# Second layer of the second block: part of the gated half's value projection moved from the input projection into the retention half, with the gate scratch moved

## Chip, cores and metric

One core of one Trainium2 chip. The metric is the device time of one execution in microseconds (us), median of the runs. The kernel computes two stacked transformer-like blocks on 256 latent tokens and 256 context tokens of width 1024; the change touches only the last layer of the second block, some 200 us before the end.

## The reference, cut to what matters

For each of its two layers the second block projects the normed tokens once (`h @ w_in`) and splits the result. Four parts feed the retention half (q, k, v and a gate branch), four the gated half (GLA: q, k, v, and a gate branch), two are low-rank gate inputs. The second layer needs no output for the context: its rows are wanted only where they feed the states.

```python
RET_W, GLA_K, GLA_V = 512, 256, 512
IN_SPLITS = (RET_W, RET_W, RET_W, RET_W, GLA_K, GLA_K, GLA_V, GLA_V, 16, 16)

def hybrid_mixer(h, hc, w_in, ...):
    lat = project_in(h, w_in)          # 256 latents
    cx = project_in(hc, w_in)          # 256 context rows
    ...
    def gla_inputs(parts):
        q = to_heads(parts[4], 4) * (64 ** -0.5)
        k = to_heads(parts[5], 4)
        v = to_heads(parts[6], 4)      # the value projection of the gated half
        a_f = to_heads(gla_log_gate(parts[8], gate_up[0], gate_b[0]), 4)
        a_b = to_heads(gla_log_gate(parts[9], gate_up[1], gate_b[1]), 4)
        return q, k, v, a_f, a_b

    r_lat, r_ctx = bidirectional_scan(retention_inputs(lat, True), retention_inputs(cx, False))
    g_lat, g_ctx = bidirectional_scan(gla_inputs(lat), gla_inputs(cx))
    return merge(r_lat, g_lat, lat), ...
```

## The kernel before

**Engines and order.** Each engine runs a program written out by hand, with semaphores between them. In layer `l` of the second block (`l` is 0 or 1, the second layer is `l == 1`) there are four phases: `l1_in` (input projection), `l1_att` (retention, then gated half), `l1_out`, `l1_mlp`. `phase_end` is a barrier of all five engines' programs except where it is told not to wait.

**Input projection.** `w_in` comes in chunks of 512 columns: chunk 0 is q, 1 is k, 2 is v, 3 the gate branch of retention, 4 q and k of the gated half, 5 its v, 6 its gate branch, and 7 the 32 low-rank columns. Products are made to nearly full precision from three matmuls of rounded operands (`mm3`: high times high, high times low, low times high). Latents and context stand side by side: `Hh` (high) and `Hl` (low, same memory as `H`) are 8 blocks of 128 features by 512 tokens, columns 0 to 255 the latents, 256 to 511 the context. Chunks 2 and 5 are made token-major: for each of four token blocks `tb` (0 and 1 are latents, 2 and 3 context) 8 x 3 matmuls of 512 columns go into one bank, and ScalarE (`take`) copies it to `RV` or `GV`. The other chunks are made feature-major, four tiles of 24 matmuls, 256 columns wide for the second layer, 512 where the context is wanted too.

**The ring.** Weights go through four slots of 2 MB. A chunk takes two: it lands in slot `n`, VectorE (`split_chunk`) casts it to the high part in slot `n+1` and writes the low part back into slot `n`, and TensorE then waits for the pair (`chunk_in`). When TensorE has used the pair, it adds 2 to the semaphore `used`; that count rides on the first matmul of the next chunk (`pend`). `load` on SyncE waits for `used` to reach `n - RING + 1`. So the load of a chunk is issued only once TensorE has begun the chunk before it, and lands and is split while that one is computed.

**Retention half.** Per head `h` (0 to 3): GpSimd makes decay arguments (`head_args`), ScalarE their exponentials (`head_exps`), VectorE scales (`head_prep`), TensorE makes the context state, scores of the next head, the intra product, the state's product and turns the next keys; ScalarE squares the head, TensorE sums it (`variance`), ScalarE and VectorE normalise. Between these stand the gate's soft-plus (`gate_soft`), its running sums (`gate_sums`, a scan), `end_exp` and `gate_exps`. TensorE runs its list in order, as all engines do. The buffers of the decay tables lie over `Hh`.

**Gated half.** `g_keys(0)` turns keys into banks 6 and 7, then scores, updates, masks, states and outputs of both directions. It reads `GV`.

Of the kernel before, what the change touches and what calls it, by code (L numbers as in the profile page):

```python
# [23 lines left out]
ALU = mybir.AluOpType  # L24
ACT = mybir.ActivationFunctionType
AX = mybir.AxisListType

P = 128
# [123 lines left out]
def build(nc, T, out):  # L152
    ctx = ExitStack()
    with ctx:
# [67 lines left out]
        END = MLP1 + 16  # L222
        WIN_ORDER = [1, 0, 3, 2, 4, 5, 6, 7, 8, 9, 10, 11]
# [70 lines left out]
        def _(sp):  # L294
# [199 lines left out]
        GT1 = [H[:, 2 * d:2 * d + 2, :] for d in range(2)]  # L494
        GLg = [H[:, 4 + 2 * d:6 + 2 * d, :] for d in range(2)]
        GQM, GQD = GT1, GLg
# [54 lines left out]
        def _(pe):  # L551
# [491 lines left out]
            for l, first, mlp in ((0, L0, MLP0), (1, L1, MLP1)):  # L1043
                W = 2 * L if l == 0 else L
                for j in range(7):
                    n = first + 2 * j
                    chunk_in(n + 1)
                    wh, wl = as_cols(n + 1, slot=low), as_cols(n, slot=low)
                    if l and j < 2:
                        wh = NextHigh(j)  # L1050
                    if j == 0:
                        o = [tile_bank() for nt in range(4)]
                        for k in range(KT):
                            if l:
                                pe.wait_ge(S("normed"), 56 + 2 * (k + 1))
                            else:
                                pe.wait_ge(S("h_split"), 8 + k + 1)
                            for nt in range(4):
                                for w in (wh, wl):
                                    mm(o[nt][:, 0:W], w[:, k, nt * P:(nt + 1) * P], Hh[:, k, 0:W], k == 0 and w is wh, False)  # L1060
                            if l:
                                pe.wait_ge(S("h_split"), 8 + 16 + k + 1)
                            for nt in range(4):
                                mm(o[nt][:, 0:W], wh[:, k, nt * P:(nt + 1) * P], Hl[:, k, 0:W], False, k == KT - 1,
                                   "tile_done" if k == KT - 1 else None)
                    elif j in (2, 5):
                        for tb in range(4):
                            o = tile_bank()
                            c = slice(tb * P, (tb + 1) * P)
                            for k in range(KT):  # L1070
                                mm3(o, (Hh[:, k, c], Hl[:, k, c]), (wh[:, k, :], wl[:, k, :]), k == 0, k == KT - 1,
                                    "tile_done" if k == KT - 1 else None)
                    else:
                        for nt in range(4):
                            wide = 2 * L if j == 1 or (j == 4 and nt >= 2) else W
# [16 lines left out]
                n = first + 14  # L1092
                chunk_in(n + 1)
                wh, wl = as_cols(n + 1, 32, slot=low), as_cols(n, 32, slot=low)
                o = tile_bank()
                for k in range(KT):
                    mm3(o[0:32, :], (wh[:, k, :], wl[:, k, :]), (Hh[:, k, :], Hl[:, k, :]), k == 0, k == KT - 1,
                        "tile_done" if k == KT - 1 else None)
                chunk_used(2)
# [19 lines left out]

                keys_turned(0)  # L1120
# [5 lines left out]
                for h in range(RT_H):  # L1126
# [42 lines left out]
                def g_scores(d, part):  # L1169
# [4 lines left out]
                    for ch in half_of(part):  # L1174
                        for h in range(4):
# [3 lines left out]
                               GQM[d][r, h // 2, ch * P:(ch + 1) * P], inc="g_scores" if h == 3 else None)  # L1179
# [15 lines left out]
                def g_inter(d):  # L1195
                    for n, ch in enumerate(order[d]):
# [3 lines left out]
                        for h in range(4):  # L1200
                            r = slice(64 * (h % 2), 64 * (h % 2) + 64)
                            mm(ps[h][:, ch * P:(ch + 1) * P], GST[d][r, n - 1, h // 2, :], GQD[d][r, h // 2, ch * P:(ch + 1) * P], False, (d, n) == (1, 3),
                               "g_out" if (d, n) == (1, 3) else None)

                g_keys(0)
# [142 lines left out]
        def _(act):  # L1348
# [281 lines left out]
            for l in range(LAYERS):  # L1630
# [13 lines left out]
                for j in range(8):  # L1644
                    for nt in range(1 if j == 7 else 4):
# [43 lines left out]
                def gate_out(d):  # L1689
                    for t in range(2):  # L1690
                        act.wait_ge(S("gate_mm"), 4 * l + 2 * d + t + 1)
                        A_(GT1[d][:, t, :], ps[(5, 1, 2, 3)[2 * d + t]][:, :], ACT.Identity, bias=vec("gate_b", l * 4 + d * 2 + t))\
# [12 lines left out]
                def gate_exps(d):  # L1705
                    link(A_(GKM[d], GT1[d], ACT.Exp, scale=-1.0 / 16))
                    A_(GQM[d], GT1[d], ACT.Exp, scale=1.0 / 16).then_inc(S("g_exp"), 1)
                    end = P - 1 if d == 0 else 0
                    link(A_(GEND[d], GLg[d].rearrange("p t (c k) -> p (t c) k", k=P)[:, :, end], ACT.Exp, scale=1.0 / 16))
                    A_(GQD[d], GLg[d], ACT.Exp, scale=1.0 / 16).then_inc(S("g_exp"), 1)  # L1710
# [20 lines left out]
                head_square(1)  # L1731
                head_exps(3)
# [6 lines left out]
                gate_exps(0)  # L1739
                head_inverse(2, 5)  # L1740
# [202 lines left out]
        def _(dve):  # L1943
# [448 lines left out]
            for l in range(LAYERS):  # L2392
# [68 lines left out]
                by_chunk = lambda a: a.rearrange("p t (c k) -> p (t c) k", k=P)  # L2461
# [11 lines left out]
                def gate_args(d):  # L2473
                    v = by_chunk(GLg[d])
                    mid, end = (63, 127) if d == 0 else (64, 0)
                    V.tensor_tensor(by_chunk(GT1[d]), v, bc(v[:, :, mid:mid + 1], [P, 8, P]), ALU.subtract)
                    V.tensor_tensor(by_chunk(GKE[d]), bc(v[:, :, end:end + 1], [P, 8, P]), v, ALU.subtract).then_inc(S("g_arg"), 1)
# [5 lines left out]
                def gate_products(d):  # L2483
# [3 lines left out]
                    V.tensor_tensor(GQM[d][:, :, 0:W], GQM[d][:, :, 0:W], GQ[:, :, 0:W], ALU.mult).then_inc(S("gq_ready"), 1)  # L2487

                def gate_queries(d):
                    dve.wait_ge(S("g_exp"), 3 * (2 * l + d) + 3)  # L2490
                    V.tensor_tensor(GQD[d][:, :, 0:W], GQD[d][:, :, 0:W], GQ[:, :, 0:W], ALU.mult).then_inc(S("gq_ready"), 1)
# [212 lines left out]
```

## Time and profile before

| | us |
|---|---|
| median of 3 runs | 1970.4 (1968.82 to 1971.67) |
| profiled execution, its own time | 1971.46 |
| its span in the trace | 1969.6 |
| TensorE busy | 1868.5 (95%) |
| VectorE / ScalarE / GpSimd busy | 818.2 / 586.1 / 387.5 |
| input projection of the second layer, TensorE's matmuls | 1553.1 to 1687.5 |
| retention half, first matmul to last variance but one | 1688.4 to 1717.2 |
| gated half, to the last output copied | 1717.2 to 1741 |

Times below are us from the span's start. The busy share of TensorE is an average over the whole program; in the retention and gated halves it is lower.

### The profile page before, as it was taken

What the parts mean: (1) busy time and instruction counts of PE and PEld (TensorE: products, weight loads), DVE (VectorE), ACT (ScalarE), POOL (GpSimd) and SP (SyncE); (2) the same over time, 40 slices, a digit from 0 to 9 for tenths busy, and PEclk for the clock granted to TensorE, in tenths of its full rate; (3) what the DMA queues carried; (4) which work ended last, traced back from release to release, by engine and by line L of the source; (5) the groups of instructions that cost most, each with busy time, mean ns of one, the idle gap of its engine ahead of it and who ended that gap; (6) DMA issues with size and microseconds to landing.
All of it is one profiled execution on the core that took longest, in us unless ns stands there. A gap on an engine that the chain in (4) does not pass through costs nothing.

```text
span 1969.6 us, 26164 instructions
## 1 busy us (share of the span) xinstructions
PE 1868.5 (95%) x11248; PEld 1366.6 (69%) x11248; DVE 818.2 (42%) x1342; ACT 586.1 (30%) x892; POOL 387.5 (20%) x205
## 2 busy tenths in 40 slices
PE   5999999999999999999999899999999899889998
PEld 2777796964444343447887657888888688679998
DVE  1615255731111111116343744566655625574333
ACT  2513103331111111113113535223333411544554
POOL 2000000120000000004003132333443210425665
PEclk8999999989999999999999899999999899999999
DMA  9479917669999999992224004454445222414451
GB/s 357 153 256 344 341 44 278 215 270 429 426 427 428 427 427 427 427 394 82 86 86 161 3 33 171 150 181 162 149 150 182 92 91 89 171 47 168 174 196 38
DMA packets 111425, 429.84 MB, mean 218 GB/s; under 512 B 5706, under 2 KB 8821, under 8 KB 98512
## 3 DMA queue, kind: packets, MB, share of 16 engines
q1 hardware_dynamic: 109056, 416.56, 54.5%
q0 software_dynamic: 2256, 11.62, 1.6%
q8 instruction: 90, 1.47, 0.3%
q14 instruction: 23, 0.19, 0.0%
HBM read 427.11 MB, written 1.05 MB: 217 GB/s over the span
## 4 chain that ended last, share of the span: by engine, by line
PE 65%; DMA 17%; DVE 5%; PEld 5%; issue 3%; ACT 3%; POOL 2%; PEldq 0%; SPq 0%; POOLq 0%; DVEq 0%; ACTq 0%
PE bank L556 64%; DMA ring<-in_moe_w_down 7%; PEld bank L556 4%; DMA H<-in_moe_w_down 4%; DMA arena<-in_moe_w_down 4%; DMA ring<-in_ada_w 2%; PE bank L571 1%; PEldq L535 0%; POOL arena L1889 0%; POOL arena L1888 0%; DVE H L1976 0%; DMA ring<-in_w_in 0%; DVE H_low L1983 0%; POOL arena L1893 0%; POOL arena L1891 0%
## 5 line engine op out<-in xcount | busy, mean ns | idle before, releaser
L556 PE MATMUL bank<-arena_r 128*128 128x256 f32 (+1 forms) x2176 | 591.7, 339 | 12.1 <-ACT arena_r L1380 6.1
L556 PE MATMUL bank<-arena_r,ring_low 128*128 128x512 f32 (+2 forms) x1920 | 596.4, 342 | 1.8 <-DVE H_low L1983 1.0
L556 PEld LDWEIGHTS bank<-arena_r 128*128 128x128 f32 x2176 | 384.9, 190 | 63.2 <-issue 18.2
L556 PE MATMUL bank<-arena 128*128 128x64 bf16 (+8 forms) x2908 | 366.1, 319 | 42.7 <-DMA arena<-in_hy_filt_w 11.7
L556 PEld LDWEIGHTS bank<-arena_r,ring_low 128*128 128x128 f32 (+1 forms) x1920 | 352.5, 188 | 47.7 <-issue 2.7
L556 PEld LDWEIGHTS bank<-arena 128*128 128x128 bf16 (+4 forms) x2908 | 206.2, 132 | 203.8 <-issue 168.6
L556 PE MATMUL bank<-H_low,arena_r 128*128 128x512 f32 (+1 forms) x672 | 217.3, 340 | 0.0
L556 PE MATMUL bank<-ring,arena 128*64 128x512 f32 x768 | 172.0, 603 | 8.4 <-DMA ring<-in_moe_w_down 7.9
L2556 DVE SCALAR_TENSOR_TENSOR X<-bank,mod,X 128x256 f32<-128x256 f32 x216 | 94.2, 478 | 196.6 <-PE bank L556 196.6
L1915 POOL TENSOR_TENSOR ring_low<-ring,arena_r 128x2048 fp32r<-128x2048 f32 x31 | 142.3, 4614 | 131.1 <-DVE ring_low L2568 69.1
L1394 ACT ACTIVATE arena<-bank 128x512 f32<-128x512 f32 (+2 forms) x106 | 51.2, 496 | 368.5 <-PE bank L556 368.5
L2329 DVE SCALAR_TENSOR_TENSOR arena_r<-bank,arena,arena_r 128x512 fp32r<-128x512 f32 x32 | 24.0, 750 | 308.6 <-ACT arena_r L1577 308.6
L1931 POOL TENSOR_TENSOR arena_r<-arena,arena_r 128x512 fp32r<-128x512 f32 (+1 forms) x64 | 104.6, 1647 | 222.5 <-ACT arena L1794 222.5
L556 PEld LDWEIGHTS bank<-ring,arena 128*64 128x64 f32 x768 | 57.1, 139 | 116.1 <-issue 115.9
L556 PEld LDWEIGHTS bank<-H_low,arena_r 128*128 128x128 f32 x672 | 125.5, 191 | 14.5
L2624 DVE SCALAR_TENSOR_TENSOR arena<-ring,arena 128x1024 f32<-128x1024 f32 x84 | 99.5, 1222 | 66.1 <-POOL arena_r L1931 62.6
L556 PE MATMUL bank<-H,arena 128*64 128x512 f32 (+4 forms) x464 | 118.4, 444 | 5.3 <-DVE arena L2514 2.7
L556 PE MATMUL bank<-X,ring 128*128 128x256 f32 x512 | 116.6, 383 | 0.0
L556 PEld LDWEIGHTS bank<-X,ring 128*128 128x128 f32 x512 | 95.4, 190 | 17.4 <-issue 4.7
L1787 ACT ACTIVATE arena_r<-ring 128x4096 fp32r<-128x4096 f32 x15 | 54.5, 3630 | 172.7 <-DMA ring<-in_w_mlp 123.7
L556 PE MATMUL bank<-H_low,ring_low 128*128 128x512 f32 (+2 forms) x272 | 93.4, 358 | 0.0
L556 PE MATMUL bank<-ring_low,arena_r 128*128 128x512 f32 x288 | 92.8, 394 | 0.0
(304 smaller groups left out, 1845.4 us busy)
## 6 DMA issues: line engine op xcount, KB each, us to landing
ring<-in_w_mlp SPq DMA_DIRECT2D x32, 2048.0 KB, 7.8
ring<-in_w_in SPq DMA_DIRECT2D x26, 2048.0 KB, 9.1
ring<-in_ada_w SPq DMA_DIRECT2D x24, 2048.0 KB, 11.6
ring<-in_moe_w_up SPq DMA_DIRECT2D x17, 2048.0 KB, 23.2
ring<-in_moe_w_gate SPq DMA_DIRECT2D x17, 2048.0 KB, 27.8
arena<-in_moe_w_up SPq DMA_DIRECT2D x15, 2048.0 KB, 22.4
ring<-in_moe_w_down SPq DMA_DIRECT2D x14, 2048.0 KB, 23.3
arena<-in_moe_w_down SPq DMA_DIRECT2D x13, 2048.0 KB, 24.3
```

Source lines behind the costliest of these rows:

```text
L556: ins = nc.tensor.matmul(o, l, r, start=start, stop=stop, skip_group_check=True)
L571: ins = nc.tensor.transpose(o, i, ident)
L1394: A_(o, i, f, **kw).then_inc(S("tile_free"), 1)
L1787: A_(W2h, slot(n), ACT.Copy).then_inc(S("w_high"), 1)
L1915: G.tensor_tensor(low(n)[:, s], slot(n)[:, s], W1h[:, s].bitcast(F32), ALU.subtract).then_inc(S("w1_split"), 1)
L1931: G.tensor_tensor(HAl[:, nt, 0:W], HA[:, nt, 0:W], HAh[:, nt, 0:W].bitcast(F32), ALU.subtract)\
L2329: V.scalar_tensor_tensor(YSl[:, s], ps[6 + nb][:, :], WSL, YSh[:, s].bitcast(F32), ALU.mult, ALU.subtract)\
L2556: i = V.scalar_tensor_tensor(X[:, t, s * L:(s + 1) * L], o[:, s * L:(s + 1) * L], mod[:, 1 + l, gate + t, s:s + 1], X[:, t, s * L:(s + 1) ...
L2624: d = V.scalar_tensor_tensor(CPROD[:, c, :], as_turned(n)[:, q % 3, :], 1.0, CSIL[:, c, :], ALU.mult, ALU.mult, accum_out=mod[:, 2, bass.d ...
```

## The change

In the second layer only:

- The chunks come in the order 0, 1, 2, 3, 4, 6, 7, 5. Chunk 5 (the gated half's values) is last, and in the input projection only its two context blocks are made. The pair of slots is kept.
- The two latent blocks are made in the retention half (`values`): per head 1 + 2 + 1 of the 8 feature blocks, so 3, 6 and 3 matmuls of 512 columns, behind the context state, behind the intra product, and behind the turned keys. Heads 0 and 1 make block 0, heads 2 and 3 block 1, both in bank 7. ScalarE copies each out (`values_out`), the first ahead of `head_exps(3)`, the second ahead of `head_inverse(2)`. `values(1, ...)` waits for the first copy, `g_keys(0)` for the second.
- Since the decay tables lie over `Hh`, ScalarE copies its latent half to `HT` (128 x 2048 numbers) after chunk 0's tiles. `Hl` has to stay as well, so the gate scratch `GT1` and `GLg` goes from `H` to the context columns of `X` and `H`: four rows of 256 in place of two of 512, and four scans of 256 per direction in `gate_sums` in place of two of 512.
- The first layer computes what it did.

```diff
+        IN_ORDER = ((0, 1, 2, 3, 4, 5, 6, 7), (0, 1, 2, 3, 4, 6, 7, 5))
+        IN_WIDE = [[2 * RANK if c == 7 else 512 for c in order] for order in IN_ORDER]
...
-                for j in range(7):
-                    load(first + 2 * j, cols(T["w_in_2"][l], j * 512, 512), as_cols(first + 2 * j))
-                load(first + 14, cols(T["w_in_2"][l], 7 * 512, 2 * RANK), as_cols(first + 14, 2 * RANK))
+                for j, c in enumerate(IN_ORDER[l]):
+                    n, w = first + 2 * j, IN_WIDE[l][j]
+                    load(n, cols(T["w_in_2"][l], c * 512, w), as_cols(n, w))
...
+        GT1_OF = ([four(H[:, 2 * d:2 * d + 2, :]) for d in range(2)], [X[:, 4 * d:4 * d + 4, L:2 * L] for d in range(2)])
+        GLG_OF = ([four(H[:, 4 + 2 * d:6 + 2 * d, :]) for d in range(2)], [H[:, 4 * d:4 * d + 4, L:2 * L] for d in range(2)])
+        HT = AR3(8192, KT, 512)[:, :, L:2 * L]
...
-                    elif j in (2, 5):
-                        for tb in range(4):
+                    elif chunk in (2, 5):
+                        for tb in range(2 if l and chunk == 5 else 0, 4):
...
-                    chunk_used(2)
+                    if not (l and chunk == 5):
+                        chunk_used(2)
...
+                def values(tb, ks):
+
+                    if l == 0:
+                        return
+                    n = first + 14
+                    if ks[0] == 0:
+                        tiles[0] += 1
+                        pe.wait_ge(S("tile_free"), tiles[0] - 1)
+                    wh, wl = as_cols(n + 1, slot=low), as_cols(n, slot=low)
+                    c = slice(tb * P, (tb + 1) * P)
+                    for k in ks:
+                        mm3(ps[7], (HT[:, k, c], Hl[:, k, c]), (wh[:, k, :], wl[:, k, :]), k == 0, k == KT - 1,
+                            "tile_done" if k == KT - 1 else None)
+                    if (tb, ks[-1]) == (1, KT - 1):
+                        chunk_used(2)
...
+                    values(h // 2, (4 * (h % 2),))
                     if h:
                         pe.wait_ge(S("gate_out"), 4 * l + h + 1)
...
+                    values(h // 2, (4 * (h % 2) + 1, 4 * (h % 2) + 2))
                     pe.wait_ge(S("r_state_out"), c + 1)
...
                     if h < RT_H - 1:
                         keys_turned(h + 1)
+                    values(h // 2, (4 * (h % 2) + 3,))
...
+                if l:
+                    pe.wait_ge(S("tile_free"), tiles[0])
                 g_keys(0)
...
+                    if l and j == 0:
+                        act.wait_ge(S("normed"), 56 + 2 * KT)
+                        A_(HT, Hh[:, :, 0:L], ACT.Copy)
...
+                def values_out(tb):
+                    if l:
+                        tile()
+                        take(GV[:, tb, :], ps[7])
...
                 head_square(1)
+                values_out(0)
                 head_exps(3)
...
                 gate_exps(0)
+                values_out(1)
                 head_inverse(2, 5)
...
-                for j in range(5, 7):
-                    split_chunk(first + 2 * j)
-                split_chunk(first + 14, KT * 2 * RANK)
+                for j in range(5, 8):
+                    split_chunk(first + 2 * j, KT * IN_WIDE[l][j])
...
-                    for t in range(2):
-                        lg, r = GLg[d][:, t, :], R128[d]
+                    rows_ = [H[:, 4 + 2 * d + t, :] for t in range(2)] if l == 0 else [GLg[d][:, q, :] for q in range(4)]
+                    for lg in rows_:
+                        r = R128[d][:, 0:2 * L // (l + 1)]
```

## Rows read from the trace of the kernel before

**Rows 1.** The page, part 1: busy time, share of the span, instructions of each engine
```profile
PE 1868.5 (95%) x11248; PEld 1366.6 (69%) x11248; DVE 818.2 (42%) x1342; ACT 586.1 (30%) x892; POOL 387.5 (20%) x205
```

**Rows 2.** Chain that ended last, second layer's projection to gated half: start, us, what
```profile
1631.17 56.37 PE bank L556 x312
...
1688.38 1.66 POOL arena L1888
...
1717.81 1.06 ACT H L1710
...
1721.76 2.35 DVE H L2470 x2
```

**Rows 3.** Timeline of ScalarE in `l1_in`: start, us, instruction, [idle before, releaser]
```profile
1576.16 0.60 ACT L1394 ACTIVATE arena<-bank 128x512 f32<-128x512 f32 x1 [9.07 <-PE bank L556]
...
1653.77 0.60 ACT L1394 ACTIVATE arena<-bank 128x512 f32<-128x512 f32 x1 [4.99 <-PE bank L556]
1659.37 0.60 ACT L1394 ACTIVATE arena<-bank 128x512 f32<-128x512 f32 x1 [5.00 <-PE bank L556]
...
1679.16 0.38 ACT L1394 ACTIVATE arena<-bank 128x256 f32<-128x256 f32 x1 [2.50 <-PE bank L556]
1682.04 0.38 ACT L1394 ACTIVATE arena<-bank 128x256 f32<-128x256 f32 x1 [2.49 <-PE bank L556]
...
1687.57 0.59 ACT L1394 ACTIVATE arena<-bank 32x512 f32<-32x512 f32 x1 [2.68 <-PE bank L556]
```

**Rows 4.** Timeline of SyncE's queue: three loads of `w_in`, each alone
```profile
1631.57 0.37 SPq L301 DMA_DIRECT2D ring<-in_w_in  x1
...
1648.41 0.37 SPq L301 DMA_DIRECT2D ring<-in_w_in  x1
...
1670.68 0.37 SPq L301 DMA_DIRECT2D ring<-in_w_in  x1
```

**Rows 5.** Timeline of VectorE in `l1_in`: casts and subtractions of `split_chunk`
```profile
1640.73 2.29 DVE L2360 CAST ring_low<-ring 128x4096 fp32r<-128x4096 f32 x1 [2.11 <-DMA ring<-in_w_in]
...
1656.12 2.29 DVE L2360 CAST ring_low<-ring 128x4096 fp32r<-128x4096 f32 x1 [8.56 <-DMA ring<-in_w_in]
1658.52 4.42 DVE L2361 TENSOR_TENSOR ring_low<-ring,ring_low 128x4096 fp32r<-128x4096 f32 x1
```

**Rows 6.** Windows: stretch, length, busy by engine (instructions), PEclk, DMA share, GB/s
```profile
1553.00:1556.00 3.00, 2.92 (x14) 2.95 (x15) 3.00 (x9) 1.65 (x5) 0.00 (x0) 0.50 0.01 3
...
1640.00:1687.00 47.00, 47.00 (x251) 38.51 (x250) 19.17 (x12) 7.57 (x13) 0.00 (x0) 1.00 0.22 74
...
1693.00:1696.00 3.00, 3.00 (x11) 2.48 (x11) 0.00 (x0) 1.06 (x3) 2.92 (x3) 0.50 1.05 388
```

**Rows 7.** Timeline of TensorE in the retention half, rows that follow idle time
```profile
1699.90 2.89 PE L556 MATMUL bank<-arena 128*128 128x128 f32 x16 [1.11 <-ACT arena L1675]
1704.48 1.13 PE L556 MATMUL bank<-arena 128*128 128x256 f32 x4 [1.69 <-ACT arena L1679]
...
1707.97 2.89 PE L556 MATMUL bank<-arena 128*128 128x128 f32 x16 [1.71 <-ACT arena L1675]
1711.56 1.13 PE L556 MATMUL bank<-arena 128*128 128x256 f32 x4 [0.71 <-ACT arena L1679]
...
1713.68 3.14 PE L556 MATMUL bank<-arena 128*128 128x128 f32 x16 [0.34 <-DVE arena L2444]
...
1720.09 1.07 PE L556 MATMUL bank<-arena,base 128*128 128x256 f32 x2 [1.80 <-ACT arena L1683]
```

**Rows 8.** Timeline of ScalarE in `l1_att`: first step of `head_inverse(2)`
```profile
1718.77 0.46 ACT L1362 ACTIVATE arena<-bank,vecs 128x256 f32<-128x256 f32 x1
```

**Rows 9.** First load of the MLP's weights: issue, us to landing, first reader
```profile
1687.76 0.38 SPq L301 DMA_DIRECT2D ring<-in_w_mlp  x1
...
ring<-in_w_mlp SPq DMA_DIRECT2D x2, 2048.0 KB, 15.6
...
1748.35 3.70 ACT L1758 ACTIVATE arena_r<-ring 128x2048 fp32r<-128x2048 f32 x2
```

More of the change, by code:

```diff
@@ L492, in build, with four, by_chunk @@
         RMU = et[:, 48:64]
-        GT1 = [H[:, 2 * d:2 * d + 2, :] for d in range(2)]
-        GLg = [H[:, 4 + 2 * d:6 + 2 * d, :] for d in range(2)]
-        GQM, GQD = GT1, GLg
+        def four(a):
+            return a.rearrange("p t (s n) -> p (t s) n", s=2)
+        GT1_OF = ([four(H[:, 2 * d:2 * d + 2, :]) for d in range(2)], [X[:, 4 * d:4 * d + 4, L:2 * L] for d in range(2)])
+        GLG_OF = ([four(H[:, 4 + 2 * d:6 + 2 * d, :]) for d in range(2)], [H[:, 4 * d:4 * d + 4, L:2 * L] for d in range(2)])
+        HT = AR3(8192, KT, 512)[:, :, L:2 * L]
+        def by_chunk(l, a):
+            return a.rearrange("p q (c k) -> p (q c) k", k=P) if l == 0 else a.rearrange("p q (c k) -> p q c k", k=P)
         GKE = [A3(0, 2, 512), A3(4096, 2, 512)]
@@ L1044, in _ @@
                 W = 2 * L if l == 0 else L
-                for j in range(7):
-                    n = first + 2 * j
+                GQM, GQD = GT1_OF[l], GLG_OF[l]
+                for j, chunk in enumerate(IN_ORDER[l]):
+                    n, wide_in = first + 2 * j, IN_WIDE[l][j]
                     chunk_in(n + 1)
-                    wh, wl = as_cols(n + 1, slot=low), as_cols(n, slot=low)
+                    wh, wl = as_cols(n + 1, wide_in, slot=low), as_cols(n, wide_in, slot=low)
                     if l and j < 2:
@@ L1065, in _ @@
                                    "tile_done" if k == KT - 1 else None)
-                    elif j in (2, 5):
-                        for tb in range(4):
+                    elif chunk == 7:
+                        o = tile_bank()
+                        for k in range(KT):
+                            mm3(o[0:32, :], (wh[:, k, :], wl[:, k, :]), (Hh[:, k, :], Hl[:, k, :]), k == 0, k == KT - 1,
+                                "tile_done" if k == KT - 1 else None)
+                    elif chunk in (2, 5):
+                        for tb in range(2 if l and chunk == 5 else 0, 4):
                             o = tile_bank()
@@ L1074, in _ @@
                         for nt in range(4):
-                            wide = 2 * L if j == 1 or (j == 4 and nt >= 2) else W
+                            wide = 2 * L if chunk == 1 or (chunk == 4 and nt >= 2) else W
                             o = tile_bank()
@@ L1091, in _ @@
                                    inc="swapped" if h % 2 else None)
[L1092 to L1099, printed above, removed]
                 flush()
@@ L1118, in variance @@
                     mm(ps[bank][:, 0:W], ones, OQ[:, h, 0:W], inc="r_var")
+                def values(tb, ks):
[9 more added lines that the diff above has]
+                        mm3(ps[7], (HT[:, k, c], Hl[:, k, c]), (wh[:, k, :], wl[:, k, :]), k == 0, k == KT - 1,
+                            "tile_done" if k == KT - 1 else None)
+                    if (tb, ks[-1]) == (1, KT - 1):
+                        chunk_used(2)
                 keys_turned(0)
@@ L1178, in g_scores @@
                             mm(ps[SB_[d] + h % 2][:, (k % 4) * P:(k % 4 + 1) * P], GKM[d][r, h // 2, ch * P:(ch + 1) * P],
-                               GQM[d][r, h // 2, ch * P:(ch + 1) * P], inc="g_scores" if h == 3 else None)
+                               GQM[d][r, 2 * (h // 2) + ch // 2, (ch % 2) * P:(ch % 2 + 1) * P], inc="g_scores" if h == 3 else None)
                 def g_updates(d):
@@ L1643, in _ @@
                 A_(lg, lg, ACT.Ln, scale=-1.0, bias=vec("one")).then_inc(S("lgam"), 1)
-                for j in range(8):
-                    for nt in range(1 if j == 7 else 4):
+                GT1, GLg = GT1_OF[l], GLG_OF[l]
+                for j in IN_ORDER[l]:
+                    for nt in range(2 if l and j == 5 else 0, 1 if j == 7 else 4):
                         o = tile()
@@ L1691, in gate_out @@
                         act.wait_ge(S("gate_mm"), 4 * l + 2 * d + t + 1)
[L1692 removed]
+                        A_(GT1[d][:, 2 * t:2 * t + 2, :], ps[(5, 1, 2, 3)[2 * d + t]][:, :].rearrange("p (s n) -> p s n", s=2), ACT.Identity, bias=vec("gate_b", l * 4 + d * 2 + t))\
                             .then_inc(S("gate_out"), 1)
@@ L1705, in gate_exps @@
                 def gate_exps(d):
-                    link(A_(GKM[d], GT1[d], ACT.Exp, scale=-1.0 / 16))
-                    A_(GQM[d], GT1[d], ACT.Exp, scale=1.0 / 16).then_inc(S("g_exp"), 1)
+                    link(A_(four(GKM[d]), GT1[d], ACT.Exp, scale=-1.0 / 16))
+                    A_(GT1[d], GT1[d], ACT.Exp, scale=1.0 / 16).then_inc(S("g_exp"), 1)
                     end = P - 1 if d == 0 else 0
-                    link(A_(GEND[d], GLg[d].rearrange("p t (c k) -> p (t c) k", k=P)[:, :, end], ACT.Exp, scale=1.0 / 16))
-                    A_(GQD[d], GLg[d], ACT.Exp, scale=1.0 / 16).then_inc(S("g_exp"), 1)
+                    ends = GEND[d] if l == 0 else GEND[d].rearrange("p (q c) -> p q c", c=2)
+                    link(A_(ends, by_chunk(l, GLg[d])[..., end], ACT.Exp, scale=1.0 / 16))
+                    A_(GLg[d], GLg[d], ACT.Exp, scale=1.0 / 16).then_inc(S("g_exp"), 1)
                 def gate_keys(d):
@@ L2460, in _, with each @@
                 nx = 4 if l == 0 else 2
-                by_chunk = lambda a: a.rearrange("p t (c k) -> p (t c) k", k=P)
+                GT1, GLg = GT1_OF[l], GLG_OF[l]
+                def each(e):
+                    return bc(e, [P, 8, P]) if l == 0 else bc(e, [P, 4, 2, P])
                 def gate_sums(d):
@@ L2473, in gate_args, with of_queries @@
                 def gate_args(d):
-                    v = by_chunk(GLg[d])
+                    v = by_chunk(l, GLg[d])
                     mid, end = (63, 127) if d == 0 else (64, 0)
-                    V.tensor_tensor(by_chunk(GT1[d]), v, bc(v[:, :, mid:mid + 1], [P, 8, P]), ALU.subtract)
-                    V.tensor_tensor(by_chunk(GKE[d]), bc(v[:, :, end:end + 1], [P, 8, P]), v, ALU.subtract).then_inc(S("g_arg"), 1)
+                    V.tensor_tensor(by_chunk(l, GT1[d]), v, each(v[..., mid:mid + 1]), ALU.subtract)
+                    V.tensor_tensor(by_chunk(l, four(GKE[d])), each(v[..., end:end + 1]), v, ALU.subtract).then_inc(S("g_arg"), 1)
+                def of_queries(a):
+                    return a if l == 0 else a.rearrange("p (t s) n -> p t s n", s=2)[:, :, 0, :]
                 def end_product(d):
```

6 lines of the change are left out of this document (3 added, 3 removed).

## Prediction

> **What bounds the kernel now.** I read the page's engine shares, then the chain that ended last through the second layer, then the engines' timelines around it. TensorE is busy 95% of the span [rows 1], but that is an average. In the input projection the chain is TensorE alone: one piece of 56.37 us from 1631.17 [rows 2], and the window from 1640 to 1687 shows 47.00 of 47.00 us busy at full clock [rows 6]. There a matmul taken out is worth its duration. In the retention half the chain leaves TensorE: it starts on GpSimd at 1688.38, goes through ScalarE and VectorE, and stands at 1717.81 on ScalarE and at 1721.76 on VectorE [rows 2]. TensorE has idle time there. So the change moves work from a stretch that it bounds into one that it doesn't. Two questions decide: what else ends the projection once 48 matmuls are gone, and how much idle time lies ahead of each place where they come back.
>
> **What is removed from the projection.** Two tiles of 24 matmuls of 512 columns. Copies of such tiles follow each other by 1659.37 - 1653.77 = 5.60 us [rows 3], so 0.233 us a matmul and 11.2 us for both.
>
> **What the new order adds there.** The last chunk is now a full one, and what stands ahead of it is the 32-column chunk. A load waits until TensorE has begun the chunk before. By time: the fifth chunk is unchanged and ends near 1648.1; its successor's first matmul lets a load go at 1648.41 [rows 4], 0.3 us after. In the new order chunk 6 runs next, four tiles of 1682.04 - 1679.16 = 2.88 us [rows 3], so 11.5 us to 1659.6; then chunk 7, 1687.57 - 1682.04 = 5.5 us [rows 3], to 1665.1. Only when chunk 7 starts can the load of chunk 5 be issued, near 1659.9 (before, the load at that point was the small one of 1670.68 [rows 4], which a chunk of 11.5 us hid). From issue to cast it took 1656.12 - 1648.41 = 7.7 us and 1640.73 - 1631.57 = 9.2 us [rows 4, 5]; cast and subtraction end 1658.52 + 4.42 - 1656.12 = 6.8 us after the cast's start [rows 5]. So the pair is ready 14.5 to 16.0 us after the issue, at 1674.4 to 1675.9, and TensorE has stood since 1665.1: a new wait of 9.3 to 10.8 us, almost all that was removed. The two context blocks then take 11.2 us: end at 1685.6 to 1687.1.
>
> **The clock after that wait.** After idle time TensorE came back at half clock: PEclk 0.50 from 1553 to 1556 [rows 6], right after the norm, that is 1.2 and not 2.4 GHz. Three us at half clock lose 1.5 us. I add that: end at 1687.1 to 1688.6, in the middle 1687.9, against a last copy that began at 1687.57 and a last matmul at 1687.5 before [rows 3]. **Projection: +0.4 us; bounds -1.9 (fast landing, clock kept) to +1.1.** The Trainium skill (TensorE: Matmul & The Clock Gate, "HAM oscillation") says the same against this change: where a burst of matmuls is shorter than the wait for its data, the next burst starts cold. The row above agrees, and without that effect the sum would be 1.5 us lower.
>
> **Other edits in the projection**, each at nothing: the copy to `HT` is one ScalarE pass of 2048 numbers, 3.70 / 2 = 1.85 us for such a size [rows 9], behind chunk 0's copies where ScalarE idles 9.07 us [rows 3]; if that cover were gone it would cost 1.85 us. VectorE's mean and column steps now stand behind the late split, ready some 5 us after it, still ahead of the end of the two blocks. The loads of `w_out` go a little earlier. The barrier's other parties wait for TensorE as before.
>
> **What comes back in the retention half.** 48 matmuls, 0.70 + 1.40 + 0.70 = 2.8 us for each head, 11.2 us. TensorE's idle time from there to head 3 is 1.11, 1.69, 1.71, 0.71 and 0.34 us, in sum 5.56 [rows 7]; up to 1699 it works without a pause. Filling is in order, so I let the pieces eat these gaps: 11.2 - 5.6 = 5.6 us are left, and `variance(2)`, done at 1717.2 before, is late by that. Who waits: `head_inverse(2)` on ScalarE, which began at 1718.77, right behind `gate_exps(0)` [rows 2, 8], so 1.5 us of the delay is hidden, and 4.1 us reaches ScalarE and then VectorE's `head_norm(2)`, the scans (2.35 us for two [rows 2]) and the masks, all of them the chain. The delay starts sooner on the same road: the keys of head 3 are turned about 2.5 us later (two thirds of the pieces, less the gaps), and ScalarE's `keys_out(3)`, `end_exp(0)` and `gate_exps(0)` stand behind one another; that shift lies within the 4.1. GpSimd isn't delayed: its third set of arguments starts after head 0 with some 4 us to spare. The idle 1.80 us at 1720.09 [rows 7] gives nothing back, since `variance(3)` waits for ScalarE's square of head 3, which stands behind `head_inverse(2)`.
>
> **Waits that are added.** `values(1, ...)` waits for ScalarE's copy of block 0 (0.60 us as in [rows 3]), which stands behind the inverse and square of heads 0 and 1; behind this wait on TensorE are the scores of head 3. I expect a stop of about 1 us, partly the gap of 1.71 that I counted. `g_keys(0)` waits for the second copy; behind it are `variance(3)` and the scores, who wait for ScalarE anyway. **Retention: +4.1 us.** Lower bound 3.0: 1693 to 1696 ran at half clock [rows 6], and if that doesn't come again about 1.1 us of the pieces is free. Upper bound 6.0: one more stretch at half clock falls on pieces and costs another 1.5 to 1.9.
>
> **Scans.** Four of 256 in place of two of 512, the same numbers; two of 512 took 2.35 us [rows 2]. The fixed part isn't visible in a row; between nothing and 0.4 us for the one on the chain, I take 0.2. The strided scratch changes no count of elements: nothing.
>
> **The MLP's first loads.** The last pair is freed on TensorE's first score of the gated half, near 1725 and not 1687.76. They took 15.6 us to land [rows 9], so about 1741, and the first reader is at 1748.35 [rows 9] plus the delay: 7 us or more of cover, at nothing.
>
> **Sum.** +0.4 + 4.1 + 0.2 = +4.7 us. The profiled execution took 1971.46, so 1976.2; it lay 1.06 above the median 1970.4, which puts the forecast at **1975.1 us**. The ends: -1.9 + 3.0 + 0 = +1.1, 1971.5; 1.1 + 6.0 + 0.4 = +7.5, 1977.9.
>
> **The rivals.** About 0.2% (3.9 us) is what a measurement of this kernel can tell from no change.
> (a) *Same mechanisms, small ends.* The load lands in 7.7 us and the clock holds at one or both places: +1.1 to +3.9, about 1973. For it: both durations are in the rows. Chance 0.28.
> (b) *The pieces are free.* TensorE's small matmuls in the retention half wait for others more than the gaps show, and everything fits: the projection's +0.4 alone, 1970.8. Against it: 11.2 us of work and 5.6 us of gaps. Chance 0.06.
> (c) *Faster: the last chunk is there in time.* One mechanism: its load and split, 14.5 to 16.0 us, hide behind chunks 6 and 7 together (17.0 us). Then the wait is gone, and the change gives -11.2 + 4.1 + 0.2, 1963.5. It decides from a wait under 11.2 - 4.3 = 6.9 us down. Against it: the count that releases the load rises with chunk 7's first matmul, as the three loads show [rows 4]. Together with faster for a cause I don't see: 0.09.
> (d) *It grows.* The delay in retention shifts GpSimd or the MLP's loads past their cover, or two half-clock stretches fall on pieces: over +7.5, about 1980. Chance 0.07.
> (e) *It doesn't do what it says*: the moved blocks end up after the retention half, because TensorE waits for the first copy long enough that all of block 1 comes late. That is (d) in time.
> Forecast: 0.50.
>
> **How the numbers follow.** Forecast and (d) are slower, but a twentieth of the forecast's band lies under 3.9: slower 0.55. (a), (b) and that part are within 0.2%: 0.36. Faster 0.09. The likeliest case alone reaches from 1974.3 to 1977.9. The range leaves out (c) and the far part of (d), and takes in (b): 1970.3 to 1978.6.
>
> **What the changed profile would show.** Chunk 5's load some 11 us ahead of the old small one, near 1659.9; a cast at 1668; TensorE idle for 9 to 11 us from 1665, released by VectorE's subtraction, with PEclk 0.5 behind it; the projection's end within 2 us of 1687.5. In the retention half no idle time on TensorE before heads 1 and 3, `head_inverse(2)` about 4 us later after the barrier than the 30.4 us of before, and everything behind shifted by the same. It would be wrong if the cast stood at 1660 or earlier, or if `head_inverse(2)` kept its distance from the barrier.

## The result, and the profile after

| | before | changed |
|---|---|---|
| median of 13 runs each, us | 1971.51 (1968.82 to 1978.54) | 1978.99 (1971.98 to 1984.93) |
| profiled execution / its span, us | 1971.46 / 1969.6 | 1975.86 / 1974.1 |
| chunk 4's first matmul to the barrier | 57.2 | 58.2 |
| barrier to `head_inverse(2)` | 30.4 | 35.7 |
| from there to the first masks | 5.4 | 5.5 |
| first masks to the cast of `w_out` | 22.4 | 22.8 |

The ratio is 1.0033 with a 95% interval of 1.0022 to 1.0044: 6.5 us slower (4.3 to 8.7); the two medians differ by 7.5. The four stretches of the table hold all that the change touches but the copy to `HT`, which stands ahead of them at 1567.4 us, took 1.93 us and has nobody waiting for it in the profile. They add up to +6.8 us; the two profiled executions differ by 4.5 alone because the changed one happened to reach chunk 4 2.3 us sooner (1628.85 against 1631.17 [rows 2]).

The page, part 1, and the chain that ended last (start, us, what), to set beside [rows 1, 2]:

```profile
PE 1868.2 (95%) x11248; PEld 1369.9 (69%) x11248; DVE 820.2 (42%) x1346; ACT 588.0 (30%) x893; POOL 387.2 (20%) x205
```

```profile
1628.85 34.01 PE bank L567 x216
1662.87 9.35 issue
1672.21 13.96 PE bank L567 x48
...
1687.42 13.50 PE bank L567 x41
...
1701.14 6.31 PE bank L567 x32
...
1715.72 6.53 PE bank L567 x33
...
1726.37 1.84 DVE H L2517 x3
```

TensorE's busy time is the same: the work moved, none went. Two things are new in the chain. The one unbroken piece of 56.37 us is now 34.01, a hole of 9.35 and 13.96. And behind the barrier the chain, which left TensorE for GpSimd, ScalarE and VectorE before, stays on TensorE all through the retention half, but for 1.7 us of ScalarE from 1708.83 that end in the copy of the first value block. The hole, in the timelines of SyncE's queue (the last chunk's load) and of VectorE:

```profile
1657.60 0.37 SPq L303 DMA_DIRECT2D ring<-in_w_in  x1
```

```profile
1665.29 2.29 DVE L2403 CAST ring_low<-ring 128x4096 fp32r<-128x4096 f32 x1 [16.09 <-DMA ring<-in_w_in]
1667.68 4.43 DVE L2404 TENSOR_TENSOR ring_low<-ring,ring_low 128x4096 fp32r<-128x4096 f32 x1
```

The load goes as chunk 7 starts, 7.7 us later the cast begins, 6.8 us later the pair is ready, 14.5 us in all, where chunk 7 gives 5.5 of cover. The windows (length, busy by engine, PEclk, DMA share, GB/s) show the clock behind the hole and in the retention half:

```profile
1672.20:1677.70 5.50, 5.49 (x13) 4.33 (x14) 4.93 (x6) 0.00 (x0) 0.00 (x0) 0.50 0.63 219
...
1691.30:1698.20 6.90, 6.90 (x20) 5.11 (x19) 1.38 (x2) 4.56 (x6) 6.72 (x6) 0.51 0.00 0
1698.20:1722.20 24.00, 23.12 (x118) 19.64 (x118) 15.56 (x26) 15.48 (x29) 10.60 (x9) 1.00 0.00 1
```

Behind its hole TensorE ran at 1.2 GHz for 5.5 us, and again for 6.8 us on end from some 4 us behind the barrier, where before it was one stretch half as long, 3.4 us, of which [rows 6] show three. The clock had already fallen inside the hole, 4.6 us after TensorE stopped, and stayed at half for 10.2 us in all. From 1698 on it is busy 23.1 of 24.0 us: the gaps of [rows 7] are full. What is left of them in the timeline of TensorE are the two waits for ScalarE's copies of the value blocks (L1425):

```profile
1710.57 0.73 PE L567 MATMUL bank<-ring_low,arena_r 128*128 128x512 f32 x2 [0.88 <-ACT arena L1425]
...
1722.92 1.09 PE L582 MATMUL bank<-base,arena 128*128 128x128 f32 x8 [0.26 <-ACT arena L1425]
```

The two marks by which every kernel is measured below are GpSimd's first instruction behind the barrier and ScalarE's first step of `head_inverse(2)`, here 1722.76 - 1687.02 = 35.7 us apart, against 1718.77 - 1688.38 = 30.4 [rows 2, 8]:

```profile
1687.02 1.67 POOL L1931 TENSOR_SCALAR arena<-arena 128x512 f32<-128x512 f32 x1 [90.10 <-ACTq L546]
```

```profile
1722.76 0.47 ACT L1393 ACTIVATE arena<-bank,vecs 128x256 f32<-128x256 f32 x1
```

### The profile page after: what moved, and what is told of

It reads as the page before. It is cut to its first block, busy times and chain, and to the rows that moved or that the text cites. A ratio compares the mean times of both kernels' runs of the same rounds, so it can differ in the third digit from the quotient of the medians.

```text
span 1974.1 us, 26169 instructions
## 1 busy us (share of the span) xinstructions
PE 1868.2 (95%) x11248; PEld 1369.9 (69%) x11248; DVE 820.2 (42%) x1346; ACT 588.0 (30%) x893; POOL 387.2 (20%) x205
## 3 DMA queue, kind: packets, MB, share of 16 engines
HBM read 427.11 MB, written 1.05 MB: 217 GB/s over the span
## 4 chain that ended last, share of the span: by engine, by line
PE 66%; DMA 17%; DVE 5%; PEld 5%; issue 3%; ACT 2%; POOL 1%; PEldq 0%; SPq 0%; POOLq 0%; DVEq 0%; ACTq 0%
PE bank L567 65%; DMA ring<-in_moe_w_down 7%; PEld bank L567 4%; DMA H<-in_moe_w_down 4%; DMA arena<-in_moe_w_down 4%; DMA ring<-in_ada_w 2%; PE bank L582 1%; DVE H L2019 0%; DMA ring<-in_w_in 0%; PEldq L546 0%; DVE arena L2549 0%; DVE H_low L2026 0%; DVE ring_low L2625 0%; DVE ring_low L2199 0%; DVE ring_low L2619 0%
## 5 line engine op out<-in xcount | busy, mean ns | idle before, releaser
L567 PE MATMUL bank<-arena_r 128*128 128x256 f32 (+1 forms) x2176 | 591.6, 339 | 10.9 <-ACT arena_r L1411 6.2
L1425 ACT ACTIVATE arena<-bank 128x512 f32<-128x512 f32 (+2 forms) x106 | 51.1, 496 | 371.2 <-PE bank L567 371.1
L567 PE MATMUL bank<-ring_low,arena_r 128*128 128x512 f32 x288 | 96.7, 408 | 10.2 <-issue 9.3
```

Source lines behind the costliest of these rows:

```text
L567: ins = nc.tensor.matmul(o, l, r, start=start, stop=stop, skip_group_check=True)
L1425: A_(o, i, f, **kw).then_inc(S("tile_free"), 1)
```

## The experiments

Four causes were weighed, two of them as full theories. **A**: the loss has two places, a wait for the last chunk that the new order makes, and pieces of the value projection that find no gap. **B**: the pieces are free, and the clock alone costs. Beside them **C** (the strided scratch costs) and **D** (the projection would not end sooner even without the wait). All kernels ran beside the kernel before on the same chip; ratios are against it.

| kernel | ratio (95%) | chunk 4 to barrier | barrier to `head_inverse(2)` | half clock (PEclk 0.50) there |
|---|---|---|---|---|
| before | 1 | 57.2 | 30.4 | 3.4 |
| changed | 1.0033 (1.0022 to 1.0044) | 58.2 | 35.7 | 6.8 |
| changed, again | 1.0021 (1.0007 to 1.0035) | 57.8 | 35.7 | 6.8 |
| e1_order | 1.0072 (1.0052 to 1.0092) | 68.5 | 30.4 | 3.4 |
| e2_scratch | 0.9996 (0.9984 to 1.0008) | 57.2 | 30.4 | 0 |
| e3_thin | 1.0011 (0.9998 to 1.0025) | 58.2 | 31.2 | 6.8 |
| e4_fill | 1.0008 (0.9991 to 1.0025) | 55.6 | 34.1 | 3.4 |
| e5_rank | 0.9963 (0.9948 to 0.9977) | 46.0 | 34.1 | 3.4 |
| e5_rank, again | 0.9956 (0.9939 to 0.9972) | 46.0 | 34.1 | 3.4 |
| e6_rank_one | 0.9979 (0.9966 to 0.9993) | 51.7 | 30.9 | 0 |
| e7_copy_first | 0.9947 (0.9933 to 0.9960) | 46.0 | 32.7 | 0 |

All columns but the ratio are us from one profile each. Where a text speaks of the clock falling once or twice in the retention half, once is 3.4 us at half clock and twice is 6.8; in the traces the 6.8 us are one unbroken stretch.

**The order alone.** Everything of the change but the move: the value blocks all stay in the projection.

```diff
-                        for tb in range(2 if l and chunk == 5 else 0, 4):
+                        for tb in range(4):
...
                 def values(tb, ks):
 
-                    if l == 0:
-                        return
+                    return
...
                 def values_out(tb):
-                    if l:
-                        tile()
-                        take(GV[:, tb, :], ps[7])
+                    return
```

The copy to `HT` and the wait ahead of `g_keys(0)` are gone too; the moved scratch stays.

> Only the order of the second layer's chunks (0, 1, 2, 3, 4, 6, 7, 5) and the moved gate scratch; all four value blocks stay in the projection, nothing is added to the retention half. Theory A (two causes: a wait for the last chunk in the projection, pieces that find no gap in the retention half): TensorE idles 9 to 11 us ahead of chunk 5 as in the changed kernel, nothing is taken out in return, so the projection ends 9.4 us later plus 1.5 to 2.8 us for the clock behind the wait: 10.9 to 12.2 us above before; the retention half from barrier to the second-last inverse takes 30.4 us as before. Rival B (the pieces are free and what is lost is the clock alone): the same wait, but the retention half, which follows the same idle stretch, grows by 1 to 3 us too. Rival C (the scratch in strided halves costs): on top of A 2 us or more in the gate's steps.

Chain of e1_order, the windows behind its hole, and its first instruction of GpSimd behind the barrier and first step of `head_inverse(2)`:

```profile
1637.38 33.98 PE bank L567 x216
1671.36 9.42 issue
1680.77 24.24 PE bank L567 x96
```

```profile
1680.80:1684.10 3.30, 3.30 (x8) 2.62 (x9) 3.27 (x2) 0.00 (x0) 0.00 (x0) 0.50 0.32 91
1684.30:1690.00 5.70, 5.70 (x26) 4.60 (x25) 1.43 (x5) 0.60 (x1) 0.00 (x0) 1.00 1.04 398
```

```profile
1705.86 1.67 POOL L1922 TENSOR_SCALAR arena<-arena 128x512 f32<-128x512 f32 x1 [100.33 <-ACTq L546]
```

```profile
1736.23 0.46 ACT L1389 ACTIVATE arena<-bank,vecs 128x256 f32<-128x256 f32 x1
```

The same hole, 9.4 us, and the projection is 11.3 us longer (68.5 against 57.2), as A said (10.9 to 12.2). Of the 11.3, 9.4 are the wait and 1.8 the clock, and this is less than in the changed kernel: 3.4 us of matmuls at half clock behind the same hole, not 5.5. The retention half takes 30.4 us, to a tenth what it took: a wait that ends 24 us ahead of the barrier costs nothing behind it. In the changed kernel it ends 14 us ahead, so this alone doesn't put B out there. By the runs it is 14 us slower (10 to 18); 11.3 lies within that, and the profile's other 6.2 us lie ahead of chunk 4, where nothing was changed.

**The scratch alone**: `e1_order` with the old order.

```diff
-        IN_ORDER = ((0, 1, 2, 3, 4, 5, 6, 7), (0, 1, 2, 3, 4, 6, 7, 5))
+        IN_ORDER = ((0, 1, 2, 3, 4, 5, 6, 7), (0, 1, 2, 3, 4, 5, 6, 7))
```

> Only the gate scratch moved (four scans of 256 for two of 512); order and value projection as before. Theory A: within 0.4 us of before, each set of scans 0.1 us longer. Rival C (the scratch costs): 2 us or more above before, seen in the gate's exponentials, subtractions and scans.

Ratio 0.9996, and the projection is again one piece (chain):

```profile
1631.41 56.37 PE bank L567 x312
```

C is out: the scratch costs nothing that can be measured (1.6 us slower at most by the interval; 0.1 us in each set of scans by the trace). The trace is 0.9 us longer than before between the first masks and the cast of `w_out` (23.3 against 22.4), but of the others with the moved scratch all but `e3_thin` (23.3) take 22.4 to 22.8 there, so the scratch by itself isn't the reason.

This run also shows what the half clock does where TensorE has gaps. It had none in the retention half, and ahead of head 1's first matmuls, the first place where [rows 7] have idle time, TensorE waited 0.32 + 2.14 us where before, with 3.4 us at half clock, it waited 1.11:

```profile
1696.64 1.13 PE L567 MATMUL bank<-arena 128*128 128x256 f32 x4 [0.32 <-ACT arena L1707]
1700.13 2.89 PE L567 MATMUL bank<-arena 128*128 128x128 f32 x16 [2.14 <-ACT arena L1703]
```

The later gaps are the same to 0.02 us. So the gaps up to head 3 add up to 5.6 us with that stretch and to 6.9 without it, and the time to `head_inverse(2)` is the same.

**Thin pieces**: the same places and waits, a third of the matmuls (the two correction products of the moved blocks are left out).

```diff
-                        mm3(ps[7], (HT[:, k, c], Hl[:, k, c]), (wh[:, k, :], wl[:, k, :]), k == 0, k == KT - 1,
-                            "tile_done" if k == KT - 1 else None)
+                        mm(ps[7], HT[:, k, c], wh[:, k, :], k == 0, k == KT - 1, "tile_done" if k == KT - 1 else None)
```

> The changed kernel, but each piece in the retention half makes one matmul of its three (16 of 48; the two correction products of the latents' value blocks are left out). Theory A: 3.7 us of pieces fit into 5.56 us of gaps, so from the barrier to the second-last inverse it takes 30.4 to 31.6 us and not 35.8; the time is 4 to 5.5 us under the changed kernel, near before or 1.5 us above. Rival B (the clock is what costs): the stretches at half clock remain, 2 us at most come back.

```profile
1690.07 1.67 POOL L1930 TENSOR_SCALAR arena<-arena 128x512 f32<-128x512 f32 x1 [90.17 <-ACTq L546]
```

```profile
1721.31 0.47 ACT L1392 ACTIVATE arena<-bank,vecs 128x256 f32<-128x256 f32 x1
```

31.2 us, 4.5 less than in the changed kernel, though the half clock lasted 6.8 us as it did there. 3.7 us of pieces all but fit into the gaps and 11.2 don't: the amount of moved work is the cause, and here the pieces, the clock and the waits for the copies cost 0.8 us together. The hole in the projection stays (9.43 us).

**A filler in the hole**: 36 needless matmuls keep TensorE at work while chunk 5 lands.

```diff
+                    if l and chunk == 5:
+                        for f in range(FILL):
+                            mm(ps[7], Hl[:, f % KT, 0:P], Hl[:, f % KT, :], inc="filled" if f == FILL - 1 else None)
                     chunk_in(n + 1)
```

> The changed kernel with 36 needless matmuls of 512 columns (8.4 us at full clock, to a free bank) ahead of the wait for chunk 5. Theory A: the chunk's arrival and the start of its matmuls don't move, but they start at full clock: the projection is 2.7 us shorter (5.5 us at half clock behind the restart in the changed kernel), the retention half stays at 34 to 36 us: 2 to 3 us under the changed kernel. Rival B: the retention half too comes back to 32 us or less, 5 us or more in all. If the filler doesn't hold the clock: no change.

Timeline of TensorE at the hole's end, and the window behind it:

```profile
1675.83 0.72 PE L568 MATMUL bank<-ring_low,arena_r 128*128 128x512 f32 x2 [1.08 <-DVE ring_low L2408]
```

```profile
1676.00:1687.00 11.00, 11.00 (x48) 8.76 (x48) 4.80 (x6) 0.60 (x1) 0.00 (x0) 1.00 0.32 116
```

Of the hole 1.08 us are left, and now the profile names what ends it, VectorE's subtraction. PEclk is 1.00 where it was 0.50, and from chunk 4 to the barrier it takes 55.6 and not 58.2 us: 2.6 us, A's 2.7. The retention half came down by 1.6 us as well, with 3.4 us at half clock in place of 6.8, a cause that A had not named. So B has a share: of the delay of 5.4 us the longer stretch is 1.6, and some 3.7 remain when the half clock lasts no longer than before. By the ratios the kernel is 4.9 us under the changed one, by its stretches 4.6; A had 2 to 3.

**The wait taken away.** The 32 low-rank columns leave the ring: they are loaded early to free columns of the arena, split there, and computed between chunks 6 and 5. The last full chunk's load then has 17.0 us of cover.

```diff
+        IN_ORDER = ((0, 1, 2, 3, 4, 5, 6, 7), (0, 1, 2, 3, 4, 6, 5))
+        TAKE_ORDER = (IN_ORDER[0], (0, 1, 2, 3, 4, 6, 7, 5))
...
+                    if l and j == 2:
+                        sp.dma_start(A3(24992, KT, 32), cols(T["w_in_2"][l], 7 * 512, 32)).then_inc(S("rank_in"), 16)
...
+                    if l and chunk == 6:
+                        pe.wait_ge(S("rank_split"), 1)
+                        rh, rl = AR3(25248, KT, 32), AR3(24992, KT, 32)
+                        o = tile_bank()
+                        for k in range(KT):
+                            mm3(o[0:32, :], (rh[:, k, :], rl[:, k, :]), (Hh[:, k, :], Hl[:, k, :]), k == 0, k == KT - 1,
+                                "tile_done" if k == KT - 1 else None)
```

> The changed kernel, but the 32 low-rank columns of the second layer are taken out of the ring (loaded early to 768 free columns of the arena, split there, computed between chunks 6 and 5). So the last full chunk's load is issued when chunk 6 begins and has 11.5 + 5.5 = 17.0 us of cover for its 14.5 to 16.0 us. Theory A: no wait of over 1 us ahead of chunk 5; from chunk 4's first matmul to the barrier 46 us (57.2 before, 58.2 in the changed kernel); the retention half keeps its 34 to 36 us to the second-last inverse; in all -11.2 + 4 to 5.8 + 0.4, 5 to 7 us under before. Rival D (the matmuls taken out of the projection were not worth their duration there, something else such as VectorE's mean step or the loads ends it): 50 us or more to the barrier, and no gain against before.

```profile
1633.85 45.19 PE bank L571 x264
```

```profile
1658.62 2.29 DVE L2414 CAST ring_low<-ring 128x4096 fp32r<-128x4096 f32 x1 [7.81 <-DMA ring<-in_w_in]
1661.02 4.43 DVE L2415 TENSOR_TENSOR ring_low<-ring,ring_low 128x4096 fp32r<-128x4096 f32 x1
```

One piece again, 45.19 us where it was 56.37 [rows 2]: the 11.2 us of two tiles, and the barrier comes 46.0 us after chunk 4. The pair is ready at 1665.5, some 2.4 us before chunk 5's first matmul. D is out. With the retention half at 34.1 the expected 5 to 7 us came as 7.3 (4.5 to 10.3) by the ratio and as 7.2 in the trace from chunk 4 to the cast of `w_out`. The second time the ratio was 0.9956.

**One block, laid by the gaps**: of `e5_rank`, only the second latent block is moved, its pieces where [rows 7] has idle time.

```diff
-                        for tb in range(2 if l and chunk == 5 else 0, 4):
+                        for tb in (0, 2, 3) if l and chunk == 5 else range(4):
...
+                    if h:
+                        values(((), (1, 2), (5,), (7,))[h])
...
+                    if h == 0:
+                        values((0,))
...
+                    if h in (1, 2):
+                        values(((), (3, 4), (6,))[h])
```

> As e5_rank, but only one latent block (the second) is moved; its 24 matmuls are laid by the measured gaps: 1 feature block after head 1's keys, 2 ahead of head 1's state product, 2 behind its variance, 1 ahead of head 2's, 1 behind its variance, 1 in head 3. Theory A: 51.6 us from chunk 4 to the barrier, and 5.6 us of pieces in 5.56 us of gaps: 30.4 to 31.6 us to the second-last inverse; in all -5.6 + 0 to 1.2, 4.4 to 5.6 us under before. Rival B (pieces cost whatever the gaps): half of the changed kernel's delay stays, 33 us, and 3 us under before.

```profile
1681.41 1.67 POOL L1944 TENSOR_SCALAR arena<-arena 128x512 f32<-128x512 f32 x1 [83.47 <-ACTq L550]
```

```profile
1712.28 0.46 ACT L1407 ACTIVATE arena<-bank,vecs 128x256 f32<-128x256 f32 x1
```

30.9 us: 5.6 us of matmuls cost the retention half 0.5. So a piece is nearly free as long as a gap takes it, and the rival of this run, that pieces cost whatever the gaps (33 us), is out. In time this is 4.1 us under before (1.4 to 6.7), and `e5_rank` 7.3 (4.5 to 10.3): the intervals overlap. By the traces, from chunk 4 to the cast of `w_out`, it is 4.8 against 7.2: the other block's 5.6 us come out of the projection in full and cost 3.2 behind the barrier, some of it perhaps because `e5_rank` had 3.4 us at half clock and this kernel none. So moving it seems to pay as well, once the projection has no wait.

**The changed kernel again**, on the same chip as the last two:

> The changed kernel once more, on the chip of these runs: 9.3 us of wait ahead of chunk 5, 58 us from chunk 4 to the barrier, 34 to 36 us to the second-last inverse (the upper end where the clock falls twice), 4.7 to 7.5 us above before.

4.1 us above before (1.4 to 6.9), just under the 4.7 to 7.5 expected; 57.8 and 35.7 us: the same two places.

**The copy ahead of the inverse**: `e5_rank` with `values_out(0)` two steps earlier on ScalarE.

```diff
                 keys_out(2)
+                values_out(0)
                 head_inverse(0, 5)
                 head_square(1)
-                values_out(0)
```

> e5_rank with ScalarE's copy of the first latent block put ahead of the inverse and square of heads 0 and 1 instead of behind them. Theory A: TensorE's 0.88 us stop ahead of head 2's first piece goes, and since TensorE sets the pace of the retention half there, the second-last inverse comes 0.5 to 0.9 us sooner after the barrier than in e5_rank at the same number of half-clock stretches (34.1 to about 33.4). Rival: ScalarE's next keys are late by the 0.6 us of the copy, and nothing is gained. In time against before: 6 to 8 us under, not to be told from e5_rank by the medians.

```profile
1678.67 1.67 POOL L1942 TENSOR_SCALAR arena<-arena 128x512 f32<-128x512 f32 x1 [77.95 <-ACTq L550]
```

```profile
1711.35 0.47 ACT L1404 ACTIVATE arena<-bank,vecs 128x256 f32<-128x256 f32 x1
```

```profile
1679.00:1712.00 33.00, 31.84 (x154) 24.73 (x152) 19.54 (x37) 22.80 (x40) 22.61 (x16) 1.00 0.00 1
```

32.7 us, 1.4 less than `e5_rank`, but PEclk was 1.00 throughout, where `e5_rank` had 3.4 us at half clock. TensorE's 0.88 us stop behind head 2's context state is gone; one of 0.90 us stands just ahead of that context state instead, on keys from ScalarE:

```profile
1698.27 1.16 PE L571 MATMUL bank<-arena 128*128 128x128 f32 x8 [0.90 <-ACT arena L1721]
```

The traces can be split there. From the barrier to that matmul it took 19.60 us here and 19.97 in `e5_rank`: of the 1.3 us that full clock gave TensorE by then, 0.9 went into the wait. From it to `head_inverse(2)` it took 13.08 and 14.13, both at full clock; 0.88 of these 1.05 us is the stop that is gone. So by these two traces the copy's new place is worth about 1 us, a little more than A's 0.5 to 0.9, and the clock the other 0.4. With one profile of each, and times whose intervals overlap, this is likely and not proven. As a whole it has the lowest ratio here, 0.9947 (0.9933 to 0.9960), 10.5 us under before where 6 to 8 were expected; `e5_rank` beside it

> e5_rank once more beside e7_copy_first: 46.0 us from chunk 4 to the barrier, 34.1 us to the second-last inverse if the clock falls once there, 35.7 if twice; 5 to 8 us under before.

gave 8.7 us (5.5 to 12.0), and the intervals overlap.

## Why the prediction was right, point by point

**The time.** The forecast of 1975.1 us started from a median of 1970.4 before. On that base the measured ratio gives 1976.9, inside the range of 1970.3 to 1978.6. The changed kernel's own median of 13 runs, 1978.99, stands 0.4 above the range, beside a before that had come out at 1971.51. The forecast of +4.7 lies inside both measured intervals (4.3 to 8.7, and 1.4 to 6.9 in the repetition). That it came so near owes something to luck: how long the half clock lasts differs between runs, and no step foresaw it.

**The wait in the projection** stands as it was worked out. I had the load at 1659.9, the pair ready 14.5 to 16.0 us later and a wait of 9.3 to 10.8; in the changed kernel's own time the load went 28.75 us after chunk 4's start (28.7 forecast), the pair took 14.5 and the wait was 9.35, the low end. `e1_order` and `e5_rank` show it from both sides: with the wait and nothing taken out +11.3, with both +1.0, with the two blocks out and no wait -11.2.

**The clock behind it** was under-sized for this kernel: 3 us at half clock taken from a row behind a shorter idle time (3.1 us), 5.5 measured, 2.75 us lost and not 1.5. But it isn't a constant. In all four profiles with the hole the half clock lasted 10.2 us and began inside the hole, 2.6 to 4.6 us after TensorE stopped, which leaves 3.4 us of it behind the hole in `e1_order`, 4.9 in the repetition and 5.5 in the changed kernel and `e3_thin`, at a loss of 1.8, 2.4 and 2.8 us. In `e1_order` the forecast's 3 us would have been nearly right. The condition that the prediction put beside its row, a burst shorter than the wait for its data, isn't met here: 34 us of matmuls ran ahead of a wait of 9.4 us, and the clock fell all the same. `e4_fill` got 2.6 us back. With the landing at its fast end (-0.7) this made +1.0 for the projection and not +0.4, inside the bounds.

**The pieces**: the forecast was 11.2 us of work less 5.6 of gaps less 1.5 of slack, +4.1; measured +5.4, and +3.7 in the kernels with 3.4 us at half clock. The step that was mis-sized is again the clock: 3.4 us more of it cost 1.6 us. I had it as a bound (6.0), not as the likeliest. With no half clock `e7_copy_first` came to +2.3, below the lower bound of 3.0, but with the copy moved, which by the split above was worth about 1 us. So the sum follows the clock: with 1.7 us more lost it gives 5.8 where 5.4 were measured, at 3.4 us of half clock 4.1 where 3.7 were. The term of the gaps is borne out from below as well, though not to the tenth: one block cost 0.5 and a third of the matmuls 0.8, where the sum gives nothing for either. The slack of 1.5 has no run of its own. That before is blind to the clock there (30.4 us with 3.4 us of it, 30.4 in `e2_scratch` with none) is the same mechanism: while TensorE had gaps the half clock cost nothing, and filling the gaps took that away too.

**Waits for the copies**: 0.88 us against "about 1". **Scans**: 0.1 against 0.2. **The copy to `HT`, the scratch, the MLP's loads**: hidden; the copy took 1.93 us against 1.85. The MLP's first two loads went out at 1725.4 and 1726.0, and everything behind the cast of `w_out` took 223.0 us in both kernels.

**The sum**: +4.7 forecast; +6.8 in the touched stretches, +6.5 by the runs. Against the forecast the clock added 1.25 us in the projection and 1.6 in the retention half; the landing gave back 0.7 and the pieces 0.4, and 0.4 came up between the first masks and the cast of `w_out`, for which the forecast had no term and where it lies within what the kernels differ by (22.4 to 23.3). The rivals: (a), small ends, had the landing right and the clock wrong; (b), free pieces, is refuted by the 3.7 us that stay in `e4_fill` and `e5_rank`, while `e3_thin` and `e6_rank_one` show how much does fit; (c), the last chunk in time, did not happen, but `e5_rank` made it happen, 7.3 us under before where its price was 6.9; of (d) the longer half clock came, but not the time over +7.5; (e) not at all.

## What to carry to other kernels

When work is moved out of a stretch that an engine bounds, look first at the loads: a reordering that puts a short step just ahead of a full-size load takes away the cover of that load, and the wait can give back all that was removed (here 9.35 of 11.2 us). Then add up the idle gaps of the place it goes to, in order, and move as much as they hold; 5.6 us of matmuls in 5.6 to 6.9 us of gaps cost 0.5, twice that cost 3.7 to 5.4. And an engine without gaps feels its clock: count half-clock time there as a cost of its own, as a span and not as one number (here 0 to 6.8 us in a stretch of 31 to 36), even where the old kernel had it for free.

## What was unexpected of the hardware

In all four profiles with the 9.4 us hole the clock was at half for 10.2 us around it. In the retention half, which begins with the same instructions in all kernels, it was at half for 6.8 us on end in the changed kernel, in its repetition and in `e3_thin`, all with the hole 14 us or less of matmuls ahead of the barrier. It was 3.4 us with the hole filled (`e4_fill`), with 24 us of matmuls behind the hole (`e1_order`), in before and in both runs of `e5_rank`, and nothing in `e2_scratch`, `e6_rank_one` and `e7_copy_first`, which have no hole. TensorE was busy when it fell: in the changed kernel for the 4.2 us ahead of it without a pause. One profile each is little; that the hole reaches over the barrier is likely by this, not shown, and kernels without a hole differ among themselves by 3.4 us of half clock, which no run here explains.

What lies ahead of chunk 4, nearly the same in all kernels, ended between 1628.85 and 1639.2 us in the profiles. So single executions can't rank these kernels. The touched stretches of one trace can, but only to about 1 us, since the clock differs in them from profile to profile.
